# Keys and values as the first block of each mixer group, the attention steps one block earlier

## The reference, cut to what matters

```
x = x + 1/2 * SwiGLU_1(RMSNorm(x))
h = RMSNorm(x)
proj = h @ w_in                       # [conv a | conv b | q | k | v | gate A | gate B]
y_a = conv_module(proj a, b)          # a*sigmoid(b), causal depthwise conv of 31 taps, LayerNorm, silu, projection
q, k = rms_norm per head (16 query heads, 4 key/value heads of 64)
y_b = window_sink_attention(q, k, v, sinks) @ attn_w_out     # chunks of 64, window of 128 plus 16 metas
x = x + (sigmoid(gA) * y_a + sigmoid(gB) * y_b) @ w_out
x = x + 1/2 * SwiGLU_2(RMSNorm(x))
```

## Time and profile before

| | us |
|---|---|
| median of 3 runs | 2357.1 |
| profiled execution, its own time | 2354.26 |
| its span in the trace | 2352.5 |
| TensorE busy | 2325.6 (99%) |
| VectorE busy | 1678.2 (71%) |
| ScalarE busy | 1242.6 (53%) |
| mixer of layer 0, blocks and attention | 380.6 to 695.6 |
| mixer of layer 1 | 1555.1 to 1863.6 |

### The profile page before, as it was taken

One profiled execution on the slowest core, in us unless ns is written; L12 is line 12 of the kernel. 1 busy time (PEld: TensorE's weight loads), 2 busy tenths in 40 slices (PEclk: granted clock), 3 DMA queues, 4 the chain that ended last, 5 costly groups with the idle time before them and its releaser, 6 DMA issues.

```text
span 2352.5 us, 43321 instructions
## 1 busy us (share of the span) xinstructions
PE 2325.6 (99%) x17809; PEld 2214.3 (94%) x17809; DVE 1678.2 (71%) x2748; ACT 1242.6 (53%) x2011; POOL 346.3 (15%) x454
## 2 busy tenths in 40 slices
PE   7999999999999999999999999999999999999999
PEld 7999999999999999999999999999888777998997
DVE  8855854899895488568778558548999855874773
ACT  8734733454455477356567347344544455762751
POOL 1101101112212211011011011011222122110110
PEclk9999999999999999999999999999999999999999
DMA  6845736676768968458458457366776698773753
GB/s 179 183 121 144 173 88 154 146 154 149 155 138 199 209 137 182 117 141 187 113 141 182 119 146 168 87 154 149 157 158 150 141 225 190 158 187 102 169 134 110
DMA packets 111365, 358.71 MB, mean 152 GB/s; under 512 B 12608, under 2 KB 12608, under 8 KB 111168
## 3 DMA queue, kind: packets, MB, share of 16 engines
q0 software_dynamic: 64080, 210.53, 44.0%
q1 hardware_dynamic: 46720, 145.08, 21.1%
q10 hardware_dynamic: 368, 0.33, 0.0%
HBM read 351.41 MB, written 2.10 MB: 150 GB/s over the span
## 4 chain that ended last, share of the span: by engine, by line
PE 89%; DVE 5%; ACT 2%; DMA 2%; issue 1%; POOL 0%; DVEq 0%; ACTq 0%
PE po L1102 28%; PE po L1119 23%; PE po L1170 21%; PE ptr L1119 7%; PE pov L1119 5%; DVE cv L1757 1%; DMA wla<-in_mixes 1%; PE pov L1349 1%; PE pov L1352 1%; PE pstat L1309 1%; DMA wha<-in_mixes 1%; PE ptr L1318 1%; PE pov L1289 0%; PE pstat L1274 0%; DVE wlb L1518 0%
## 5 line engine op out<-in xcount | busy, mean ns | idle before, releaser
L1102 PE MATMUL po<-xh,wha 128*128 128x264 f32 (+1 forms) x1408 | 345.5, 312 | 2.7 <-DMA wla<-in_mixes 2.0
L1102 PE MATMUL po<-xl,wha 128*128 128x264 f32 (+1 forms) x1408 | 335.5, 305 | 0.0
L1102 PE MATMUL po<-xh,wla 128*128 128x264 f32 (+1 forms) x1408 | 334.8, 304 | 0.0
L1757 DVE SCALAR_TENSOR_TENSOR cv<-ub,lp,cv 128x528 f32<-128x528 f32 (+1 forms) x480 | 333.3, 753 | 1.7
L1170 PE MATMUL po<-hh,wla 128*128 128x264 f32 (+1 forms) x1232 | 283.7, 300 | 0.0
L1170 PE MATMUL po<-hl,wha 128*128 128x264 f32 (+1 forms) x1232 | 283.7, 300 | 0.0
L1170 PE MATMUL po<-hh,wha 128*128 128x264 f32 (+1 forms) x1232 | 282.6, 299 | 0.4 <-DVE wla L1526 0.4
L675 ACT ACTIVATE wla<-wha 128x1024 fp32r<-128x1024 f32 x136 | 143.8, 1059 | 222.2 <-DMA wha<-in_mixes 222.1
L1526 DVE TENSOR_TENSOR wla<-wfa,wha 128x768 fp32r<-128x768 f32 (+1 forms) x128 | 113.8, 890 | 202.0 <-ACT wha L713 201.9
L1102 PEld LDWEIGHTS po<-xh,wha 128*128 128x128 f32 x1408 | 226.8, 188 | 22.1 <-issue 3.8
L713 ACT ACTIVATE wha<-wfa 128x768 fp32r<-128x768 f32 (+1 forms) x128 | 101.0, 789 | 265.7 <-DMA wfa<-in_outs 265.7
(11 more groups left out here) (240 smaller groups left out, 5676.4 us busy)
## 6 DMA issues: line engine op xcount, KB each, us to landing
wha<-in_mixes POOLq DMA_DIRECT2D x136, 512.0 KB, 4.3
wla<-in_mixes POOLq DMA_DIRECT2D x136, 512.0 KB, 6.4
raw<-in_pairs SPq DMA_DIRECT2D x88, 768.0 KB, 5.6
wfa<-in_outs SPq DMA_DIRECT2D x64, 384.0 KB, 3.1
wlb<-in_pairs POOLq DMA_DIRECT2D x47, 512.0 KB, 8.3
raw<-in_pairs SPq DMA_DIRECT2D x88, 256.0 KB, 6.9
wla<-in_pairs POOLq DMA_DIRECT2D x87, 256.0 KB, 6.6
wfa<-in_outs SPq DMA_DIRECT2D x64, 320.0 KB, 2.9
```

Source lines behind the costliest of these rows:

```text
L1102: ins = mm(po[:, 2 * out_slot + h, 0:width], w[:, k, :], v[:, k, t:t + width], start=begin and k == 0 and p == 0, stop=last and k == kt - ...
L1757: stt(cv[:, j, a:], u, w, cv[:, j, a:], ALU.mult, ALU.add).then_inc(conv_step, 1)
```

## The change

Keys and values become block i = 0 of each group, the query blocks i = 1 and 2. Steps on all engines are put one block earlier from `query_stats` on; `head_stats` goes from the end of block 3 to the end of block 1, `query_stats` from the middle of block 4 to the middle of block 3. F(2) and V(2) come into block 10 of their own group. The table `TAPS` is rewritten so that the taps fall at other blocks. The output projection of the attention is no longer cut in two.

```diff
-TAPS = (9, 8, 7, 6, 7, 8, 3, 7, 4, 5, 8)
-LATE = 9
+TAPS = (8, 6, 9, 7, 8, 3, 7, 4, 5, 8, 7)
...
-    if i < 2:
-        return "w_in", ((O_Q + (2 * g + i) * P, P),)
-    if i == 2:
+    if i == 0:
         return "w_in", ((O_K + HD * g, HD), (O_V + HD * g, HD))
+    if i < 3:
+        return "w_in", ((O_Q + (2 * g + i - 1) * P, P),)
...
             def square_q(l, g, j):
-                act.wait_ge(out_taken, tile(l, T_MIX) + g * GB_N + j + 3)
+                act.wait_ge(out_taken, tile(l, T_MIX) + g * GB_N + j + 4)
...
                     h(0)
-                    if spill:
-                        take_metas(l, g - 1, 2)
+                    act.wait_ge(out_taken, tile(l, T_MIX) + g * GB_N + 3)
+                    func(t0[0:HD, :], kvp[0:HD, PAD:], ACT.Square).then_inc(ksq_ready, 1)
+                    h(1)
                     square_q(l, g, 0)
-                    if spill:
-                        take_o(l, g - 1, 2)
-                    h(1)
+                    head_std(l, g)
+                    h(2)
                     square_q(l, g, 1)
-                    h(2)
-                    act.wait_ge(out_taken, tile(l, T_MIX) + g * GB_N + 2 + 3)
-                    func(t0[0:HD, :], kvp[0:HD, PAD:], ACT.Square).then_inc(ksq_ready, 1)
                     h(3)
-                    head_std(l, g)
+                    query_std(l, g)
                     fill_tanh(l, g, 3)
                     h(4)
-                    query_std(l, g)
                     fill_tanh(l, g, 4)
+                    for i in range(SB):
+                        attn_exp(l, g, 0, i)
                     h(5)
                     fill_tanh(l, g, 5)
-                    for i in range(SB):
-                        attn_exp(l, g, 0, i)
                     h(6)
+                    take_windows(l, g, 0)
                     fill_tanh(l, g, 6)
-                    h(7)
-                    take_windows(l, g, 0)
-                    fill_tanh(l, g, 7)
                     for i in range(SB):
                         attn_exp(l, g, 1, i)
-                    h(8)
+                    h(7)
                     take_metas(l, g, 0)
...
-                    mids = {4: do(lambda: query_stats(l, g)), 7: do(lambda: S(1)), 8: do(lambda: F(0)), 9: do(lambda: L(1)), 10: do(lambda: V(1))}
-                    ends = {3: do(lambda: head_stats(l, g)), 5: do(lambda: S(0)), 7: do(lambda: L(0)),
-                            8: do(lambda: V(0), lambda: S(2)), 9: do(lambda: F(1)), 10: do(lambda: L(2))}
-                    if g:
-                        mids[0] = do(lambda: F(2, before))
-                        ends[0] = do(lambda: V(2, before))
-                    else:
+                    mids = {3: do(lambda: query_stats(l, g)), 6: do(lambda: S(1)), 7: do(lambda: F(0)),
+                            8: do(lambda: L(1)), 9: do(lambda: V(1)), 10: do(lambda: F(2))}
+                    ends = {1: do(lambda: head_stats(l, g)), 4: do(lambda: S(0)), 6: do(lambda: L(0)),
+                            7: do(lambda: V(0), lambda: S(2)), 8: do(lambda: F(1)), 9: do(lambda: L(2)),
+                            10: do(lambda: V(2))}
+                    if g == 0:
                         mids[0] = do(lambda: stat(l, 1))
...
             def attn_out_start(l):
-                g = GROUPS - 1
+                def tile_ready(k):
+
+                    if k == KD - 2:
+                        pe.wait_ge(o_lo, (l + 1) * GROUPS * NBAT + 1)
                 for m in range(2):
                     free(l, T_ATT + m)
-                    products(l, B_ATT + m, ps(m), KD - 2, ah, al, last=False, done=False, post=l == LAST,
-                             mid=(lambda: turn_first(l, g, 2)) if m == 0 else None)
-                    if m == 0:
-                        mix_values(l, g, 2)
-                pe.wait_ge(o_lo, (l + 1) * GROUPS * NBAT + 1)
-                for m in range(2):
-                    products(l, B_ATT + m, ps(m), KD, ah, al, begin=False, k0=KD - 2, post=l == LAST)
+                    products(l, B_ATT + m, ps(m), KD, ah, al, before=None if m else tile_ready, post=l == LAST)
...
-                        if i == 1 and g:
+                        if i == 0 and g:
                             o_lo_part(l, g - 1, 2)
+                        if i == 1:
+                            head_rms(l, g)
                         if i == 3:
-                            head_rms(l, g)
+                            query_rms(l, g)
                         if i == 4:
-                            query_rms(l, g)
+                            row_max(l, g, 0)
                         if i == 5:
-                            row_max(l, g, 0)
-                        if i == 6:
                             norm_p(l, g, 0)
...
+                o_lo_part(l, GROUPS - 1, 2)
```

More of the change, by code:

```diff
@@ L529, in short @@
         def short(l, g, i):
-            return l == LAST and (i < 2 or i > 2 and FILL[g][i - 3][0] in (GA, GB))
+            return l == LAST and (i in (1, 2) or i > 2 and FILL[g][i - 3][0] in (GA, GB))
         @block.sync
@@ L978, in h @@
                         neg(l, B_MIX + g * GB_N + i + 3)
-                    spill = g > 0
-                    if spill:
-                        take_windows(l, g - 1, 2)
                     if g == 0:
@@ L984, in _ @@
                         neg(l, B_MIX + 2)
-                    h(0)
-                    if spill:
-                        take_metas(l, g - 1, 2)
+                    else:
+                        take_o(l, g - 1, 2)
+                    h(0)
+                    act.wait_ge(out_taken, tile(l, T_MIX) + g * GB_N + 3)
+                    func(t0[0:HD, :], kvp[0:HD, PAD:], ACT.Square).then_inc(ksq_ready, 1)
+                    h(1)
                     square_q(l, g, 0)
-                    if spill:
-                        take_o(l, g - 1, 2)
-                    h(1)
+                    head_std(l, g)
+                    h(2)
                     square_q(l, g, 1)
-                    h(2)
-                    act.wait_ge(out_taken, tile(l, T_MIX) + g * GB_N + 2 + 3)
-                    func(t0[0:HD, :], kvp[0:HD, PAD:], ACT.Square).then_inc(ksq_ready, 1)
                     h(3)
-                    head_std(l, g)
+                    query_std(l, g)
                     fill_tanh(l, g, 3)
                     h(4)
-                    query_std(l, g)
                     fill_tanh(l, g, 4)
+                    for i in range(SB):
+                        attn_exp(l, g, 0, i)
                     h(5)
                     fill_tanh(l, g, 5)
-                    for i in range(SB):
-                        attn_exp(l, g, 0, i)
                     h(6)
+                    take_windows(l, g, 0)
                     fill_tanh(l, g, 6)
-                    h(7)
-                    take_windows(l, g, 0)
-                    fill_tanh(l, g, 7)
                     for i in range(SB):
                         attn_exp(l, g, 1, i)
-                    h(8)
+                    h(7)
                     take_metas(l, g, 0)
-                    fill_tanh(l, g, 8)
+                    fill_tanh(l, g, 7)
                     take_o(l, g, 0)
@@ L1020, in _ @@
                     attn_exp(l, g, 2, 2)
+                    h(8)
+                    fill_tanh(l, g, 8)
+                    take_metas(l, g, 1)
                     h(9)
+                    take_o(l, g, 1)
                     fill_tanh(l, g, 9)
-                    take_metas(l, g, 1)
+                    take_windows(l, g, 2)
                     h(10)
-                    take_o(l, g, 1)
+                    take_metas(l, g, 2)
                     fill_tanh(l, g, 10)
-                g = GROUPS - 1
-                take_windows(l, g, 2)
-                take_metas(l, g, 2)
-                take_o(l, g, 2)
+                take_o(l, GROUPS - 1, 2)
                 def block_hi(n):
@@ L1361, in mixer_in @@
                     S = lambda b, gg=g: scores(l, gg, b)
-                    before = g - 1
                     def do(*steps):
                         return lambda: [f() for f in steps]
-                    mids = {4: do(lambda: query_stats(l, g)), 7: do(lambda: S(1)), 8: do(lambda: F(0)), 9: do(lambda: L(1)), 10: do(lambda: V(1))}
-                    ends = {3: do(lambda: head_stats(l, g)), 5: do(lambda: S(0)), 7: do(lambda: L(0)),
-                            8: do(lambda: V(0), lambda: S(2)), 9: do(lambda: F(1)), 10: do(lambda: L(2))}
-                    if g:
-                        mids[0] = do(lambda: F(2, before))
-                        ends[0] = do(lambda: V(2, before))
-                    else:
+                    mids = {3: do(lambda: query_stats(l, g)), 6: do(lambda: S(1)), 7: do(lambda: F(0)),
[4 more added lines that the diff above has]
+                    if g == 0:
                         mids[0] = do(lambda: stat(l, 1))
@@ L1762, in take @@
                 ready(l, B_MIX + n)
-                if i < 2:
-                    dst = qb[:, :, i]
```

(28 more changed lines are left out.)

1 line of the change is left out of this document (removed).

## The result

The changed kernel takes 2403.8 us (median of 4 runs, 2397.7 to 2404.2) against 2357.4 us for the kernel before. The ratio that is on record for the fast runs is 1.0187, with a 95% interval of 1.0174 to 1.0200; the two medians alone give 1.0197. Forecast were 2377.1 us, 20.0 more than before, with a range to 2388. The sign was right, but 46 us came, more than twice the size. The profiled execution takes 2397.74 us, 43.5 more than the one of before.

What follows compares the result with a forecast made beforehand. TensorE, busy 99%, was taken as the bound, with only its waits moving: stalls 22.2 + group 0 0.6 - weights 1.1 - metas 1.7 = +20.0 us, so 2374.3 profiled, median 2377.1; 8-in-10 range 2367 to 2388.

Steps and rivals of the forecast that it cites:

- The bound: Whole kernel: TensorE, busy 99%, sets the time; its work stays the same, so only its waits can move.
- The second query block: Groups 1 to 3: query_stats waits for this block's square, 3.54 us in layer 0 and 3.86 in layer 1.
- H: Start of head_stats in a group, the zero from which the prediction counted times; query_stats wanted at H + 10.99 in layer 0.
- drain: Skill's rule, weighed and not followed: about 1.38 us more at every ScalarE table switch, which would make the sum 28.3.
- Group 0, weights, metas: Group 0 waits 0.3 us per layer at query_stats; weight waits lose 1.1 us, waits on turned metas 1.7.
- the late exponentials: Batch 1 exponentials behind a tanh, now in all groups, could add 5.7 us; the stall gives VectorE time, so -1.7.
- 3 x 3.54 + 3 x 3.86 = 22.2 us: Six TensorE stalls at query_stats, groups 1 to 3: 3.54 us each in layer 0, 3.86 in layer 1.
- rival B: Each of six long stalls is followed by a slow start of 2.21 us, 13.3 in all, so 2390; 12%.
- The rule of the Trainium skill that spoke against the change: TensorE: an idle engine falls to 1.2 GHz and must work its way back; the six stalls exceed any earlier mixer wait.
- D: Tanh in block 6 delays the exponentials in every group: +7.4 us against the sum, 2384.5; 7%.

Runs made afterwards that it cites:

- run 1: Changed kernel with no taps at block 1 (6 before) and 15 at block 2 (9 before): 2381.6 us, ratio 1.0099.
- run 5: Kernel before, order unchanged, plus a TensorE wait ahead of query_stats in groups 1 to 3 for the keys' reciprocal: 2373.7 us, ratio 1.0067.
- run 9: Kernel before plus a TensorE wait in the middle of block 6 of groups 1 to 3, for the first of 8 taps: 2368.4 us, ratio 1.0045.
- run 11: Changed kernel with only the table of taps altered, to (8, 0, 10, 7, 8, 3, 8, 5, 5, 9, 9): 2361.2 us, ratio 1.0010.
- run 2: Changed kernel with 4 taps at block 1 (6 before) and 11 at block 2 (9 before): 2390.4 us, ratio 1.0144.
- run 7: Changed kernel with no taps at block 1, 15 at block 2, and block 6's tanh behind the exponentials of batch 1: 2372.6 us, ratio 1.0062.
- run 8: Changed kernel with taps (8, 0, 10, 7, 8, 3, 8, 5, 5, 9, 9), keys' root before first query square, batch 1 exponentials before tanh: 2355.0 us, ratio 0.9990.
- run 4: Kernel before plus a TensorE wait ahead of query_stats in groups 1 to 3, for a VectorE tap: 2400.1 us, ratio 1.0183.
- run 10: Kernel before plus a TensorE wait in the middle of block 6 of groups 1 to 3, for the third tap: 2378.2 us, ratio 1.0092.

## Why the prediction was wrong

*The bound.* Half right. TensorE's work stayed the same and its waits moved, but they were not all that could move: the same matmuls took 21.6 us more of busy time.

*The second query block.* Right, and close. The rows that it counts from are those of group 2; group 1 has the same lengths (10.90 us from `query_stats` to S(0), against 10.89), so the sum stands. `query_stats` was to be ready at H + 14.53 in layer 0 and H + 14.39 in layer 1. It began at H + 14.78, 14.56, 14.78 and at 14.80, 14.60, 14.81. The chain of waits of the changed kernel runs over the very steps that were added up:

```profile
559.80 1.28 ACT L939
561.08 0.01 issue
561.10 0.71 ACT t L939
561.80 0.02 issue
561.83 3.45 DVE t L1783
...
570.78 0.63 DVE qb L1764
571.41 0.02 issue
571.43 0.69 ACT pw L970
572.12 0.04 issue
572.17 3.48 PE pov L1281 x18
```

The root begins at 561.10, 3.49 us after H (557.61), forecast 3.36; the reciprocal at 4.22, forecast 4.09. The long waits add up to 23.2 us, forecast 22.2. No drain shows behind the table load: it ends at 559.80 + 1.28 = 561.08, and the root begins at 561.10.

*Group 0, weights, metas.* 0.3 us of wait in one layer, 0.3 forecast in each. The two waits on weights in group 0 are gone, 1.1 us as forecast; a new one of 0.3 elsewhere leaves 0.8 in the view. Those on the metas fell by 1.6 (1.7). That the stall would hide the late exponentials was right too: in run 1, without the stall, they were late.

*The step that failed* is the term "3 x 3.54 + 3 x 3.86 = 22.2 us" of the sum: it took each stall at its own length and put what lies behind it at nothing. The lengths were right (23.2 us), but the matmuls behind each stall also ran slower, by 3.2 to 4.6 us each, 21.9 us, about as much as the waits themselves. This was rival B, with 12%. Two things were misjudged. The evidence against B, that waits of 1.5 us had left no mark, was taken from other places, while the new ones stand in front of 18 or 16 matmuls of 2 columns; run 5 shows that there even 1.3 us is enough, and in the profile of run 9 it was not elsewhere. And B's price, 2.21 us from the first matmuls of the program, was too low for stretches of low clock that lasted 6.8 us in four places and 10.2 in two, so that even B's 2390 fell 13.8 us short. The rule of the Trainium skill that spoke against the change ("TensorE: Matmul & The Clock Gate", "Part 1: The HAM clock gate") was the better guide than the missing mark. The Trainium skill speaks of an idle engine; in run 5 TensorE was idle for only 1.3 us, with the narrow matmuls right behind.

*D and the range.* D was right in its mechanism and hidden here. The range left out most of B on purpose; the time lay 16 us above it.

## What to carry to other kernels

A new wait of a TensorE-bound kernel is to be priced twice: its length, and what the matmuls behind it lose while the granted clock is low, here as much again. Look at what stands next to the wait: beside a run of narrow matmuls a wait of 1.3 us was enough each time, amid wide ones waits of 1.15 to 1.87 us left it up in one profile, and waits of 2.5 to 3.6 us brought the clock down in three places of six. That the narrow matmuls are the reason is likely, but no run shows it. And when steps are moved by a block, the filler work between them, here the taps on VectorE, has to be spread anew from each deadline: two numbers of that table were worth some 21 us, six of them some 42 (by the ratios of runs 1 and 11).

## What the runs showed of the hardware

The granted clock as tenths in 40 slices is too coarse: it shows full speed in all of these kernels. Windows of some 4 us show it, and so does the distance of two equal matmuls.

Amid wide matmuls a wait of this size can bring it down too. In a later projection of layer 1 TensorE waits for VectorE (`resid`), with matmuls of 512 columns before and behind. In runs 2, 7 and 8 the clock fell there at a wait of 1.76 to 1.85 us; in runs 4, 10 and 11 a wait of 1.77 or 1.78 left it up. This is run 8:

```profile
1988.69 0.50 PE L1094 MATMUL po<-mh,wha 128*128 128x512 f32 x1 [1.76 <-DVE resid L1727]
```
```profile
1990.00:1995.00 5.00, 5.00 (x17) 0.72 0.37 51
```

TensorE counts as busy in `query_stats`, and yet the clock can fall behind it with hardly a wait. In run 11 this stood in group 2 of layer 1:

```profile
1739.23 1.95 PE L1281 MATMUL pov<-halves,pw 128*128 128x2 f32 x16 [0.17 <-ACT pw L970]
1741.04 0.62 PE L1094 MATMUL po<-xh,wha 128*128 128x512 f32 x1
...
1746.16 0.40 PE L1094 MATMUL po<-xh,wha 128*128 128x512 f32 x1
```

and its windows:

```profile
1736.00:1740.00 4.00, 3.83 (x21) 1.00 0.50 137
1740.00:1744.00 4.00, 4.00 (x18) 0.65 0.90 199
1744.00:1748.00 4.00, 4.00 (x17) 0.92 0.20 25
```

The wait is 0.17 us. In the same run it fell in group 0 of layer 1 behind a wait of 0.22 us, and in group 3 of layer 0 behind a `query_stats` that waited for nothing that the profile shows. Each time it stayed low for 3.4 us; half of that, three times, is an estimate of 5.1 of the 7.0 us of rest. All ten runs of run 11 have a mean clock of 0.997 or 0.998, those of the kernel before on that chip 0.998 to 1.000. In the kernel before the eight places of `query_stats` never brought it down in the profiled run. What makes the difference is open; no run took the narrow matmuls away or moved them.
